# Self attention of a two-block transformer: weights left unscaled, sums from columns of ones, the inverse multiplied in on GpSimd

## What is computed

```python
def fox_attention(q, k, v, log_f):
    ...
        s = jnp.einsum('bqhd,bkhd->bhqk', q_i, k).astype(jnp.float32) * scale
        s = s + c_i[..., :, None] - c_keys[:, :, None, :]
        s = jnp.where((k_pos[None, :] <= q_pos[:, None])[None, None], s, NEG_INF)
        p = jax.nn.softmax(s, axis=-1)
        return jnp.einsum('bhqk,bkhd->bqhd', p.astype(v.dtype), v)

        o_f = rms_norm(o_f.reshape(B, S, FOX_WIDTH), g_fox_out[l])
        o_c = rms_norm(o_c.reshape(B, S, CHUNK_WIDTH), g_chunk_out[l])
        mix = jnp.concatenate([o_f, o_c], axis=-1) @ w_out[l]
```

## Time and profile before

| what | value |
|---|---|
| median of three runs | 2093.66 us (2092.72 to 2097.09) |
| span of the profiled execution, first to last instruction | 2090.6 us |
| TensorE busy in it | 2054.0 us (98%) |
| VectorE, ScalarE, GpSimd busy | 1120.3, 875.4, 964.1 us |
| chain that ended last: TensorE, VectorE, ScalarE, GpSimd | 82%, 6%, 4%, 4% of the span |
| self attention, first exponential to last product | about 162 to 269 us |

### The profile page before, as it was taken

How to read it: one execution, slowest core, us unless ns; L and a number is a source line. 1 busy time by engine, 2 the same in 40 slices (tenths; PEclk the granted TensorE clock), 3 DMA queues, 4 the chain that set the end, 5 groups by cost and what they waited for, 6 DMA issues and landing times.

```text
span 2090.6 us, 28050 instructions
## 1 busy us (share of the span) xinstructions
PE 2054.0 (98%) x9901; PEld 1688.7 (81%) x9901; DVE 1120.3 (54%) x1769; ACT 875.4 (42%) x1493; POOL 964.1 (46%) x489
## 2 busy tenths in 40 slices
PE   9999999999999999999999999999999999999997
PEld 7877787888888888787778888888777888888887
DVE  4525834335677776763385543434566635434345
ACT  5326864455222222534386322323476653232233
POOL 3437885453445545334235244444445752444443
PEclk9999999999999999999999999999999999999999
DMA  6530052214466664364323133332322031332332
GB/s 214 193 101 21 11 202 91 81 41 161 157 225 213 227 229 155 101 221 161 86 51 106 51 101 93 97 100 91 91 81 81 1 101 52 100 99 92 100 93 89
DMA packets 70325, 238.40 MB, mean 114 GB/s; under 512 B 7776, under 2 KB 11232, under 8 KB 70112
## 3 DMA queue, kind: packets, MB, share of 16 engines
q1 hardware_dynamic: 70240, 237.26, 35.4%
HBM read 231.20 MB, written 2.10 MB: 112 GB/s over the span
## 4 chain that ended last, share of the span: by engine, by line
PE 82%; DVE 6%; ACT 4%; POOL 4%; issue 3%; DMA 1%; DVEq 0%; SPq 0%; ACTq 0%; POOLq 0%
PE bank L942 25%; PE bank L944 25%; PE bank L943 25%; PE bank L1049 1%; PE bank L1176 1%; PE bank L1091 1%; POOL WL L806 1%; POOL sq L854 1%; PE bank L1064 1%; POOL t L854 1%; DVE bank L2508 1%; DVE acc L2394 1%; PE bank L1255 0%; POOL CW L879 0%; DVE x L2512 0%
## 5 line engine op out<-in xcount | busy, mean ns | idle before, releaser
L806 POOL TENSOR_TENSOR WL<-stage,WH 128x1024 fp32r<-128x1024 f32 x256 | 633.4, 2475 | 888.4 <-ACT WH L1675 883.1
L1675 ACT ACTIVATE WH<-stage 128x1024 fp32r<-128x1024 f32 x256 | 271.4, 1061 | 812.5 <-PE bank L944 799.9
L942 PE MATMUL bank<-H,WH 128*128 128x512 f32 (+1 forms) x1132 | 438.0, 387 | 2.6 <-DVE H L2418 2.1
L944 PE MATMUL bank<-H,WL 128*128 128x512 f32 (+1 forms) x1132 | 437.1, 386 | 0.0
L943 PE MATMUL bank<-H,WH 128*128 128x512 f32 (+1 forms) x1132 | 437.0, 386 | 0.0
L2757 DVE TENSOR_TENSOR Y<-bank,Y 128x512 f32<-128x512 f32 x328 | 215.6, 684 | 94.9 <-PE bank L944 94.2
L942 PE MATMUL bank<-HID,WH 128*128 128x512 f32 (+1 forms) x688 | 264.3, 384 | 0.1
L943 PE MATMUL bank<-HID,WH 128*128 128x512 f32 (+1 forms) x688 | 264.2, 384 | 0.0
L944 PE MATMUL bank<-HID,WL 128*128 128x512 f32 (+1 forms) x688 | 264.2, 384 | 0.0
L942 PEld LDWEIGHTS bank<-H,WH 128*128 128x128 f32 x1132 | 212.6, 188 | 47.9 <-issue 3.4
L944 PEld LDWEIGHTS bank<-H,WL 128*128 128x128 f32 x1132 | 212.6, 188 | 42.9
(11 more groups left out here) (468 smaller groups left out, 3612.2 us busy)
## 6 DMA issues: line engine op xcount, KB each, us to landing
stage<-panels SPq DMA_DIRECT2D x296, 512.0 KB, 3.6
ahead<-ada SPq DMA_DIRECT2D x102, 512.0 KB, 5.3
RAW<-panels SPq DMA_DIRECT2D x18, 512.0 KB, 4.0
apiece<-ada SPq DMA_DIRECT2D x10, 512.0 KB, 5.3
x<-xT SPq DMA_DIRECT2D x3, 1024.0 KB, 7.4
CS<-QKH SPq DMA_DIRECT2D x18, 128.0 KB, 2.4
outT<-x SPq DMA_DIRECT2D x16, 128.0 KB, 1.7
CS<-QKL SPq DMA_DIRECT2D x12, 128.0 KB, 2.4
```

Source lines behind the costliest of these rows:

```text
L806: pool.tensor_tensor(low_of(p, slot), stage[:, slot, :], high_of(p, slot).bitcast(F32), ALU.subtract).then_inc(s_split, 1)
L942: pe.matmul(out, wh, rh, start=start, stop=False)
L944: return pe.matmul(out, wl, rh, start=False, stop=stop)
L1675: act.activation(high_of(p, slot), stage[:, slot, :], ACT.Copy).then_inc(s_hisplit, 1)
```

## The change

The weights are no longer divided by their sum before they are turned. The exponential is taken without the row sum; reciprocal and scaling go, in the self attention alone. Instead the held columns of a head are its 64 value columns and 64 columns of ones (new buffer VO, laid out as values, ones, values, so that the even head takes the first 128 columns and the odd head the last 128). The product then has 64 rows of unscaled outputs and 64 rows that all hold the sum. VectorE copies the outputs to Y (`out` is now on VectorE); ScalarE takes the logarithm of the sums (`total_log`) into rstd, or logs for the last pair, and once both heads of a pair are there one exponential of the negated logarithm gives the inverse for both (`inverse`). GpSimd multiplies it in (`normalise`). A bank is free for the next head when both the logarithm and the copy are done. All squares of the norms go from ScalarE to GpSimd (`norm_square`, `head_square`), and VectorE's additions stand one or a few steps later. What waited for the heads to be copied now waits for them to be normalised. At the very start VectorE fills the columns of ones and zeros. The memory kept for GpSimd-issued transfers is made smaller, to make room for VO.

```diff
+        VO = place(156, "VO", [P, 2, 2, NT, 3, CH], F32R)
...
-                "v_high", "v_split", "scores", "max", "exp", "recip", "probs", "turned",
-                "pt_high", "pt_split", "pv") + (("out",) if name == "self" else ())}
+                "v_high", "v_split", "scores", "max", "exp", "turned", "pt_high", "pt_split", "pv")
+                + (("inverted", "out", "normed") if name == "self" else ("recip", "probs"))}
...
-                return staged_v(V[:, :, u // 4 * S + u % 4 * P:u // 4 * S + u % 4 * P + P], u % 2, P)
+                src = V[:, :, u // 4 * S + u % 4 * P:u // 4 * S + u % 4 * P + P]
+                return (src.rearrange("p a (h d) -> p a h d", d=CH), VO[:, u % 2, 0, :, 0:3:2, :], VO[:, u % 2, 1, :, 0:3:2, :])
...
+        def logs_done(n):
+            return 3 * (n // 2) + n % 2 + 1
+        def inverse_done(pair):
+            return 3 * pair + 3
+        def inverse_of(pair):
+            return logs if pair == 7 else rstd
...
-            sp.wait_ge(att["self"]["out"], 16)
+            sp.wait_ge(att["self"]["normed"], 8)
...
-                    if name == "self":
-                        if s >= 12 and s % 8 == 7 and s // 8 + 1 < 8:
-                            low_v(name, s // 8 + 1)
-                        continue
+            def norm_square(name, m, source, width):
+                if m >= 2 or name != "mem":
+                    pool.wait_ge(s_add, first_of(ADD, name) + max(m - 1, 0))
+                pool.tensor_tensor(nsq[:, m % 2, 0:width], source, source, ALU.mult).then_inc(s_sq, 1)
+            def self_attention():
+                sm = att["self"]
+                def normalise(pair):
+                    pool.wait_ge(sm["inverted"], inverse_done(pair))
+                    pool.wait_ge(sm["out"], 2 * pair + 2)
+                    pool.tensor_tensor(Y[:, pair, :], Y[:, pair, :], inverse_of(pair)[:, :], ALU.mult).then_inc(sm["normed"], 1)
+                def head_square(name, m):
+                    pool.wait_ge(sm["normed"], m + (5 if name == "chunk" else 1))
+                    norm_square(name, m, Y[:, m + (4 if name == "chunk" else 0), :], S)
+                low_v("self", 0)
+                low_v("self", 1)
+                for s in range(64):
+                    if s >= 15 and s % 8 == 7 and s // 8 + 1 < 8:
+                        low_v("self", s // 8 + 1)
+                    if s >= 16 and s % 8 == 0:
+                        normalise(s // 8 - 2)
+                    if 28 <= s < 36:
+                        if s == 28:
+                            pool.wait_ge(s_mem, 32)
+                        norm_square("mem", s - 28, memc(s - 28), MEM)
+                    if s in (36, 37, 39, 41):
+                        head_square("fox", (36, 37, 39, 41).index(s))
+                    if s in (49, 57):
+                        head_square("chunk", (s - 49) // 8)
+                for pair in (6, 7):
+                    normalise(pair)
+                    head_square("chunk", pair - 4)
...
-            attention("self")
+            self_attention()
...
-                    pe.wait_ge(sm["probs"], s + 1)
+                    pe.wait_ge(sm["exp" if name == "self" else "probs"], s + 1)
...
+                            pe.wait_ge(sm["inverted"], logs_done(n - 2))
...
-                    return three(O[n % 2][:, kb * P:S], VS[:, slot, 0, kb * P:(kb + 1) * P],
-                                 VS[:, slot, 1, kb * P:(kb + 1) * P], high[:, kb, kb * P:S], low[:, kb, kb * P:S],
+                    if name == "self":
+                        held = [VO[:, slot, hl, kb, n % 2:n % 2 + 2, :].rearrange("p h d -> p (h d)") for hl in range(2)]
+                    else:
+                        held = [VS[:, slot, hl, kb * P:(kb + 1) * P] for hl in range(2)]
+                    return three(O[n % 2][:, kb * P:S], held[0], held[1], high[:, kb, kb * P:S], low[:, kb, kb * P:S],
...
-            def norm_square(name, m, source, width):
-                if m >= 2 or name != "mem":
-                    act.wait_ge(s_add, first_of(ADD, name) + max(m - 1, 0))
-                act.activation(nsq[:, m % 2, 0:width], source, ACT.Square).then_inc(s_sq, 1)
...
-                if 28 <= s < 36:
-                    if s == 28:
-                        act.wait_ge(s_mem, 32)
-                    norm_square("mem", s - 28, memc(s - 28), MEM)
-                if s in (36, 37, 39, 40):
-                    m = (36, 37, 39, 40).index(s)
-                    act.wait_ge(att["self"]["out"], 2 * m + 2)
-                    norm_square("fox", m, Y[:, m, :], S)
-                if s in (47, 55, 63):
-                    m = (s - 47) // 8
-                    act.wait_ge(att["self"]["out"], 2 * m + 10)
-                    norm_square("chunk", m, Y[:, 4 + m, :], S)
...
+                    if name == "self":
+                        act.activation(prob[b][:, 0:w], score_bank(name, s)[:, 0:w], ACT.Exp, bias=stat[:, b:b + 1])\
+                            .then_inc(sm["exp"], 1)
+                        return
...
-                def out(n):
+                def total_log(n):
-                    if name == "self":
-                        act.activation(Y[half_rows[n % 2], n // 2, :], O[n % 2][half_rows[n % 2], :], ACT.Copy)\
-                            .then_inc(sm["out"], 1)
+                    if 2 <= n < 14:
+                        act.wait_ge(sm["normed"], n // 2)
+                    act.activation(inverse_of(n // 2)[half_rows[n % 2], :], O[n % 2][half_rows[1 - n % 2], :], ACT.Ln)\
+                        .then_inc(sm["inverted"], 1)
+                def inverse(pair):
+                    act.wait_ge(sm["inverted"], logs_done(2 * pair + 1))
+                    act.activation(inverse_of(pair)[:, :], inverse_of(pair)[:, :], ACT.Exp, scale=-1.0)\
+                        .then_inc(sm["inverted"], 1)
...
+                    if name == "self" and s >= 16 and s % 8 == 0:
+                        inverse(s // 8 - 2)
-                            out(2 * (s // 8 - 1) + s % 2)
+                            total_log(2 * (s // 8 - 1) + s % 2)
...
-                    out(heads - 2)
-                    out(heads - 1)
+                    inverse(6)
+                    total_log(heads - 2)
+                    total_log(heads - 1)
+                    inverse(7)
...
-            act.wait_ge(att["self"]["out"], 16)
-            norm_square("chunk", 3, Y[:, 7, :], S)
...
+                    if c == 0:
+                        act.wait_ge(att["self"]["normed"], 8)
...
-                if s in (37, 39, 40):
-                    norm_add("fox", (36, 37, 39, 40).index(s), acc, S)
+                if s in (38, 40, 43):
+                    norm_add("fox", (0, 38, 40, 43).index(s), acc, S)
...
-                if s in (56, 63):
-                    norm_add("chunk", (56, 63).index(s) + 1, acc_chunk, S)
+                if s == 60:
+                    norm_add("chunk", 1, acc_chunk, S)
...
-                maximum(0)
-                maximum(1)
-                invert(0)
-                maximum(2)
-                invert(1)
-                maximum(3)
-                invert(2)
+                def out(n):
+                    rows = half_rows[n % 2]
+                    dve.wait_ge(sm["pv"], weighed(name, n, 3))
+                    dve.tensor_copy(Y[rows, n // 2, :], O[n % 2][rows, :]).then_inc(sm["out"], 1)
+                for s in range(4):
+                    maximum(s)
+                    if s and name != "self":
+                        invert(s - 1)
-                    if s + 3 < steps:
+                    if s + 3 < steps and name != "self":
+                    if name == "self" and s >= 12 and s % 8 in (6, 7):
+                        out(2 * (s // 8 - 1) + s % 2)
...
+                if name == "self":
+                    for n in range(heads_of(name) - 2, heads_of(name)):
+                        out(n)
+                    norm_add("chunk", 2, acc_chunk, S)
...
+            for slot in range(2):
+                dve.memset(VO[:, slot, 0, :, 1, :].bitcast(F32), 1.0)
+                dve.memset(VO[:, slot, 1, :, 1, :].bitcast(F32), 0.0)
...
-            dve.wait_ge(att["self"]["out"], 16)
+            dve.wait_ge(att["self"]["normed"], 8)
...
-    nc = bacc.Bacc("TRN2", target_bir_lowering=False, num_devices=1)
+    nc = bacc.Bacc("TRN2", target_bir_lowering=False, num_devices=1, dynamic_dma_scratch_size=1024)
```

## The result

The changed kernel takes 2111.24 us (median of four runs, 2109.14 to 2115.26) against 2093.4 us: a ratio of 1.0083, 95% interval 1.0068 to 1.0098. It is **slower by 17.8 us**, where 6.0 were forecast, and 2111.24 lies outside the range. The profiled execution took 2109.14 us, its span is 2107.4 us, 16.8 us above that of before. It was the fastest of the four: the two slowest, 2113.0 and 2115.26, show a lower mean granted clock (0.991 and 0.990 against 0.994), so the median holds about 2 us that the trace doesn't have.

The account below looks back on a forecast made before the run. TensorE, busy 2054.0 of 2090.6 us, was taken as the bound; 2090.6 - 2.6 gains + 8.6 loss = 2096.6 us span, plus 3.1 to the median: 2099.7 us, 0.29% slower, range 2093.9 to 2103.5.

Parts of the forecast that it names:

- The cap: Self attention: no version issuing the same matmuls saves over 9.2 us, TensorE's 7.5 us idle plus 1.7 us low clock.
- stretch (a): 174.0 to 209.1 us: TensorE no longer waits for GpSimd's scaling; 1.2 us gained, bounds 0 and 1.76.
- (d): 209.1 to 223.1 us: VectorE waits for GpSimd's squares, one addition collides; 0.5 us lost, bounds -2.1 and +1.5.
- the layout of steps 28 to 38: All four engines' rows laid side by side: step 38 comes when it came before, 0 us without the collision.
- (e): 223.1 to 237.0 us: step 46 comes sooner after step 38, less a collision; 0.5 us gained, bounds -0.5 and +2.1.
- (c): 237.0 to 249.5 us: VectorE busy some 11.3 of 12.5 us; 0.4 us gained, bounds 0 and 0.65.
- (b): 249.5 to 262.1 us: the same waits for GpSimd's scaling go; 0.7 us gained, bounds 0 and 1.45.
- (f): 262.1 to 269.1 us, attention's end, ScalarE held by the first ring panel: 0.3 us gained, bounds -0.5 and 1.7.
- the three signs: Wrong if: keys' gap under 5 us; TensorE idle to attention's end falls over 6 us or grows; an unnamed wait appears.
- The wait at the keys: After the attention, TensorE waits for GpSimd's panel split behind the last normalisations and squares: 6.9 us, bounds 6.4 and 8.4.
- All later work starts later by that: After the keys, everything shifts by the 8.6 us loss; no later stretch has TensorE idle time to absorb it.
- Rival 2: Attention: nothing is won, VectorE stands where GpSimd stood; 0 with the 8.6 us loss gives 2102.3 us; chance 0.15.

Follow-up runs that it names:

- one wait on TensorE: Changed kernel with TensorE waiting for one semaphore instead of two ahead of heads 2 to 15, VectorE's copy waiting for the logarithm; 2106.11 us, 1.0066.
- The first experiment: Changed kernel with GpSimd's low parts of mem_k's first two panels made before the normalisation of the last two head pairs; 2101.81 us, 1.0034.

## Why the prediction failed, point by point

**The cap and stretch (a) held.** Every idle microsecond up to 209 us was won: 1.8, where 1.2 was taken, at the bound of 1.76. There was no TensorE wait over 0.3 us there.

**(d), 209 to 223: the sign was right, the size was not.** -4.0 us against -0.5, and outside the bound of -2.1. Both collisions came where they were placed, 1.1 us each instead of 1.3; VectorE's rows, to be read beside 1.66 and 0.68 in the earlier trace rows:

```profile
210.00 0.43 DVE L2662 TENSOR_TENSOR acc_mem<-nsq 128x256 f32<-128x256 f32 x1 [1.52 <-POOL nsq L889]
...
215.29 1.48 DVE L2662 TENSOR_TENSOR acc_mem<-acc_mem,nsq 128x256 f32<-128x256 f32 x1 [1.11 <-POOL nsq L889]
...
232.85 1.76 DVE L2662 TENSOR_TENSOR acc<-acc,nsq 128x512 f32<-128x512 f32 x1 [1.03 <-POOL nsq L889]
...
276.65 2.74 DVE L2662 TENSOR_TENSOR acc_chunk<-acc_chunk,nsq 128x512 f32<-128x512 f32 x1 [2.34 <-POOL nsq L889]
```

GpSimd's product runs from 215.21 to 216.49 and from 232.77 to 234.06. The rule of the Trainium skill (SBUF — State Buffer, Who interferes with whom), that the two exclude each other for whole instructions, agrees with these rows, with the 2.74 us beside a split, and with the untouched bank readers above. **The step that failed is the layout of steps 28 to 38**, which put the 14 us of these steps at no loss but 0.5 us for the collision. The kernels split its 4.0 us: the early low parts' kernel needs 17.1 us for these steps and has no wait at 211 us, since its memory landed 0.9 us sooner (GpSimd's first square at 207.90 against 208.78 us): some 1.0 us of the 4.0 is a late landing. With one wait on TensorE the steps take 15.5 us with the same squares on GpSimd and the same wait at 217 us, but its clock stays at 1.00 where the kernel with the early low parts has

```profile
210.00:220.00 10.00, 7.65 (x39) 5.60 (x40) 8.18 (x17) 5.09 (x11) 5.17 (x7) 0.88 0.00 1
220.00:230.00 10.00, 9.35 (x68) 7.60 (x66) 7.16 (x16) 7.60 (x17) 2.98 (x4) 0.95 0.01 2
```

that is 0.12 and 0.05 of 10 us each, so 1.7 us of clock, and it covers the 1.6 us between the two kernels. What is left, 15.5 - 14.0 = 1.5 us, is the queue and the collision that I had costed at 0.5. I had priced no clock loss in the middle and let the load of the memory cost what it cost before. The kernel reached it 1.8 us earlier, and the load didn't come earlier by as much (the first square started at 209.21 us before, at 208.78 now).

**(e), (c), (b)**: +0.5 was forecast for (e), -0.5 came; for (c) and (b) 0.4 and 0.7 were forecast and 0.2 and 0.6 came. In (c) VectorE was busy for 12.37 of the 12.5 us, not 11.3. Its copies take 0.67 to 0.70 us, not 0.6, and its scaling of the memory collides too (1.40 and 1.39 us at 244.79 and 257.39, 0.47 alone), which I hadn't laid out.

**(f), the end**: -1.4 against +0.3, by the wait that no row named, 2.21 us at 268.31. TensorE was idle for 2.7 us from step 62 to the end, for 0.01 before; the low clock of before (0.76) did not come there (1.00), or the loss would have been greater. I had looked at the ring panel on ScalarE's queue and not at who waits behind it: a bank now comes free by two engines, and VectorE's copy stands behind its low part. The changed order at the end removed it.

So the attention ended 3.4 us later instead of 2.6 earlier: 6.0 of the 10.8 us missed in the span. TensorE's idle time from 174 us to the attention's last matmul grew from 7.5 to 10.8 us. That and the wait named by no row are two of the three signs that I had given for being wrong.

**The wait at the keys held**: 6.43 against 6.9, the bound being 6.4, by the chain as told. GpSimd's part of it, to be read beside the earlier trace rows:

```profile
274.12 1.31 POOL L899 TENSOR_TENSOR Y<-Y,logs 128x512 f32<-128x512 f32 x1 [1.33 <-ACT logs L1987]
275.51 1.04 POOL L889 TENSOR_TENSOR nsq<-Y 128x512 f32<-128x512 f32 x1
276.51 5.12 POOL L820 TENSOR_TENSOR WL<-stage,WH 128x1024 fp32r<-128x1024 f32 x2
```

The square takes 1.04 us, not 1.29. The first experiment showed that the wait was avoidable. The low clock behind it took 2.1 us by 340 us instead of 1.7, within its bounds; the keys began at 0.50, as forecast.

**"All later work starts later by that" failed.** 4.7 us arose behind 340 us. 1.5 of them is the clock, low for twice as long around 1010 us as in before; of the fourteen experiments' traces one shows that too (the kernel before with 14 waits, 2.1 us), the others at most 0.5, so it looks like chance of single executions; no run settles it. Most of the other 3.2 (3.0, by the kernel with one wait) follows from 14 instructions on TensorE, which I had counted as free. I had also added 3.1 us from span to median. The part outside the first and last instruction is 1.7 us in the changed kernel (2109.14 - 2107.4); the other 2.1 of its 3.8 us are the distance of the median from the profiled execution.

**The rivals**: none was this case. Rival 2, nothing won, gave 2102.3; its mechanism, VectorE standing where GpSimd stood, was the one at work from 209 us on, and the attention did worse than win nothing.

## What to carry to other kernels

Where work moves between engines, follow each instruction behind the moved one in *both* queues to the engine that ends last; the worst loss here was two panel splits behind a chain they had no part in, and moving one call gave 9.4 us back (6.6 by the spans). A wait of over a microsecond on TensorE costs itself and, in about half of the cases in these traces, another 1.7 us of low clock. When a change loses time where no line was touched, compare transfer landings and the number of instructions per engine before looking for a cause in the data flow.

## What the runs showed of the hardware

A wait on TensorE that is always met has a price far from its place: 14 of them (28064 instead of 28050 instructions) moved two panel landings by about a microsecond each, some 900 and 1450 us later, and without them the changed kernel's trace lost 3.0 us less there. The clock's losses come in like portions. Between 1000 and 1030 us a stretch of 10 us has a granted clock of 0.83, so 1.7 us lost, in ten of the sixteen traces; four have the same loss spread over two stretches, and two have twice as much. The same 0.83 follows many of the pauses. On GpSimd a product with both inputs from one tile is quicker (1.04 us for 128x512) than one of two tiles (1.29), and both than the scaling with one input and a scalar per partition (1.575). VectorE's copy of 64 rows out of a bank takes as long (0.67 us) as a maximum over 128 (0.68).
